# Feed forward in steps of four blocks with half-contraction weight loads, and late attention outputs made transposed

## The reference

```
for layer in range(2):
    x = x + mixer(rms_norm(x))                    # layer 0: sliding window + latent (MLA); layer 1: dilated
    x = x + memory_cross_attention(rms_norm(x), rms_norm(mem))
    x = x + (silu(h @ w_gate) * (h @ w_up)) @ w_down     # h = rms_norm(x); hidden width 2816
return rms_norm(x)
```

## Time and profile before

| | us |
|---|---|
| Median of 3 runs | 3666.4 (3652.03 to 3669.24) |
| The profiled execution | 3675.72 |
| Its span, first to last instruction | 3673.9 |

### The profile page before, as it was taken

How to read it: one execution, slowest core, us unless ns; L and a number is a source line. 1 busy time by engine, 2 the same in 40 slices (tenths; PEclk the granted TensorE clock), 3 DMA queues, 4 the chain that set the end, 5 groups by cost and what they waited for, 6 DMA issues and landing times. The chain is left out here.

```text
span 3673.9 us, 45086 instructions
## 1 busy us (share of the span) xinstructions
PE 3154.4 (86%) x17286; PEld 2315.8 (63%) x17286; DVE 2008.6 (55%) x4183; ACT 708.2 (19%) x1736; POOL 1343.8 (37%) x1166
## 2 busy tenths in 40 slices
PE   8889988977778787577888887889998999999999
PEld 3566478843334343254667776677875788877887
DVE  2341355489898888777776688776544210133201
ACT  2231221222121111113220013210023210122100
POOL 0840032156776777653455555455300000000000
PEclk9998999988889889877899999899999999999999
DMA  6422100289999999976899999899831244422343
GB/s 216 129 75 72 46 3 5 66 295 357 367 370 358 385 371 393 357 275 232 285 344 390 393 386 347 298 349 390 330 95 35 69 143 155 139 91 81 115 149 103
DMA packets 420396, 832.17 MB, mean 227 GB/s; under 512 B 40467, under 2 KB 258510, under 8 KB 420174
## 3 DMA queue, kind: packets, MB, share of 16 engines
q0 software_dynamic: 147456, 536.94, 39.1%
q1 hardware_dynamic: 272726, 292.35, 24.3%
HBM read 827.02 MB, written 2.17 MB: 226 GB/s over the span
## 5 line engine op out<-in xcount | busy, mean ns | idle before, releaser
L2822 PE MATMUL banks<-arena 128*128 128x256 f32 (+1 forms) x4736 | 1078.7, 387 | 63.6 <-DMA arena<-in_l_w_up 32.7
L2822 PEld LDWEIGHTS banks<-arena 128*128 128x128 f32 (+1 forms) x4736 | 909.6, 194 | 218.3 <-DMA arena<-in_l_w_up 36.3
L2369 POOL DMA_INDIRECT arena<-in_peer_v,arena x512 | 583.9, 1140 | 399.9 <-DVE arena L2485 233.8
L2369 POOL DMA_INDIRECT arena<-in_peer_u,arena x512 | 571.8, 1117 | 425.6 <-DVE arena L2499 147.4
L2499 DVE CUSTOM_DVE_ANT_0 arena<-arena 128x1024 f32<-128x1024 f32 x512 | 628.2, 1227 | 114.0 <-DMA arena<-in_peer_u,arena 72.1
L2441 PE MATMUL banks<-arena 128*128 128x512 f32 x768 | 419.3, 689 | 189.0 <-DMA arena<-in_peer_v,arena 67.9
L2485 DVE SCALAR_TENSOR_TENSOR arena<-arena 128x1024 f32<-128x1024 f32 x316 | 406.2, 1286 | 31.6 <-DMA arena<-in_peer_v,arena 13.1
L2441 PEld LDWEIGHTS banks<-arena 128*128 128x128 f32 x768 | 159.9, 219 | 405.2 <-issue 314.2
L3787 PE MATMUL banks<-arena 128*128 128x256 f32 x1408 | 310.5, 378 | 0.0
L3836 DVE TENSOR_TENSOR arena<-banks,arena 128x512 f32<-128x512 f32 x44 | 30.5, 693 | 498.3 <-PE banks L2822 495.6
L3787 PEld LDWEIGHTS banks<-arena 128*128 128x128 f32 x1408 | 265.7, 189 | 38.3
(11 more groups left out here) (313 smaller groups left out, 3416.6 us busy)
## 6 DMA issues: line engine op xcount, KB each, us to landing
arena<-in_l_w_gate SPq DMA_DIRECT2D x44, 1024.0 KB
arena<-in_l_w_up SPq DMA_DIRECT2D x44, 1024.0 KB
arena<-in_l_w_down SPq DMA_DIRECT2D x44, 1024.0 KB
arena<-in_ada_w SPq DMA_DIRECT2D x24, 1024.0 KB, 7.6
arena<-in_l_w_qkv SPq DMA_DIRECT2D x24, 1024.0 KB
arena<-in_w_in SPq DMA_DIRECT2D x33, 512.0 KB, 4.0
arena<-in_l_w_out SPq DMA_DIRECT2D x16, 1024.0 KB
arena<-in_peer_q_w SPq DMA_DIRECT2D x10, 1024.0 KB
```

The lines of the kernel that those rows point to most:

```text
L2369: p.e.indirect_dma_start(e.ring[slot], None, tables[table], bass.IndirectOffsetOnAxis(ap=e.IDX[h][:, t, j:j + 1], axis=0)).then_inc(*p.up( ...
L2822: ins = p.e.matmul(out, left(c), right(c), start=c == 0, stop=c == c_n - 1, skip_group_check=True)
```

## The change

The feed forward goes in steps of blocks: (0), (1,2), (3,4), ... (9,10). For a step of two blocks, gate and up weights come as two loads each: rows 0 to 511 and rows 512 to 1023 of 512 columns (runs of 2 KB). Gate uses banks 0 and 1, up banks 2 and 3. The order is g0 u0 | g12 u12 d0 | g34 u34 d1 d2 | ... | d9 d10. Silu is written to `a.hid[i % 4]` and multiplied in place; `a.sg` goes.

In half 1 the units have an order of their own (`late_order`). The outputs of both heads of a pair are made together after the weights of the next pair's first unit, with the values stationary (64 columns, or 128 for the cross attention) and the transposed weights moving, into partitions 0 to 63 and 64 to 127 of bank 5: the result is already transposed. The reciprocal of the sum is spread over partitions by a matmul of the broadcast column with the identity into bank 4, ACT copies it to `a.O`, DVE multiplies bank 5 with it straight into `a.o`. The transposing store, DVE's scaling per unit and its copy go.

```
-        a.hid, a.sg = F.take(2, T), F.take(T)
+        a.hid = F.take(4, T)
...
+def late_order(units):
+    n, former = len(units), None
+    yield "scores", 0
+    for u in range(n):
+        paired = both_halves(units, u + 1)
+        if u + 1 < n and not paired:
+            yield "scores", u + 1
+        yield "fill", u
+        if paired:
+            yield "scores", u + 1
+        yield "weights", u
+        if units[u].c0 == 0 and former is not None:
+            yield "outputs", former
+        if units[u].ends:
+            former = u
+        yield "pause", u
+    yield "rest", 0
+    yield "outputs", former
...  (units_pe)
+        elif step == "outputs":
+            if filled < 4 * MM:
+                occupied(k, p, a, 1, 5)
+            p.wait_ge(*x.values_at)
+            p.claim(("bank", 5), S.dve_stored, key)
+            group = group_of(units, u)
+            for v in group:
+                p.wait_ge(weights_by(k, a, v), (name, v))
+            for j in range(len(x.values)):
+                for v in group:
+                    y = units[v]
+                    ins = p.e.matmul(k.bank[5][y.c0:y.c0 + y.w, 0:P], y.values[j], a.PT[v % 2][:, j * P:j * P + P], start=j == 0,
+                                     stop=j == len(x.values) - 1, skip_group_check=True)
+                    if j == len(x.values) - 1:
+                        ins.then_inc(*p.up(S.output_filled, (name, v)))
+            p.wait_ge(S.vector_step, ("inverted", *key))
+            p.claim(("bank", 4), S.act_scaled, key)
+            for v in group:
+                y = units[v]
+                ins = p.e.matmul(k.bank[4][y.c0:y.c0 + y.w, 0:P], a.small[:, v % 4, 4:5].to_broadcast([P, y.w]), k.ident,
+                                 start=True, stop=True, skip_group_check=True)
+            ins.then_inc(*p.up(S.store_filled, key))
...  (units_act)
+        elif step == "outputs":
+            if x.tile in stored:
+                p.wait_ge(S.dve_stored, stored[x.tile])
+            p.wait_ge(S.store_filled, key)
+            p.e.activation(a.O[x.tile], k.bank[4][:, 0:P], ACT.Copy).then_inc(*p.up(S.act_scaled, key))
+            stored[x.tile] = key
...  (units_dve)
+        elif step == "weights" and a.late:
+            if weights_by(k, a, u) is S.dve_weights:
+                if u >= 2:
+                    p.wait_ge(S.output_filled, (name, u - 2))
+                p.wait_ge(S.weights_filled, key)
+                p.e.tensor_copy(a.PT[1][:, 0:x.m], k.bank[4][:, 0:x.m]).then_inc(*p.up(S.dve_weights, key))
+            p.wait_ge(S.weights_exp, key)
+            if x.sink is not None or 0 < x.nb < x.m:
+                p.e.tensor_tensor(cols[:, 2:3], cols[:, 2:3], cols[:, 3:4], ALU.add).then_inc(*p.up(S.vector_step))
+                p.in_order()
+            p.e.reciprocal(cols[:, 4:5], cols[:, 2:3]).then_inc(*p.up(S.vector_step, ("inverted", *key)))
+        elif step == "outputs":
+            p.wait_ge(S.output_filled, key)
+            p.wait_ge(S.act_scaled, key)
+            p.e.tensor_tensor(x.dst, k.bank[5][:, 0:P], a.O[x.tile], ALU.mult).then_inc(*p.up(S.dve_stored, key))
...
+FFN_STEPS = [(0,)] + [(2 * q + 1, 2 * q + 2) for q in range((NH // 2 - 1) // 2)]
+GATE, UP = (0, 1), (2, 3)
+def rows_half(w, c0, r):
+    return lambda slot: [(slot.rearrange("p (c n) -> p c n", n=T), columns(w, c0, T)[:, 4 * r:4 * r + 4, :])]
...  (ffn_sp)
+            for r in range(2):
+                load_wide(k, p, (name, l, h, step[0], r), rows_half(w, 256 * step[0], r), over=(name, l, h, step[-1], r))
...
+def quad_pe(k, p, a, l, name, step, banks, emptied, norm):
+    for r in range(2):
+        w = landed_wide(k, p, (name, l, h, step[0], r)).rearrange("p (c n) -> p c n", n=T)
+        for x in range(4):
+            i, b = step[x // 2], banks[x // 2]
+            if r == 0 and x % 2 == 0:
+                p.claim(("bank", b), emptied, (l, h, i))
+            for c in range(4):
+                p.wait_ge(S.normed, (norm, 4 * r + c))
+                ins = p.e.matmul(k.bank[b][:, x % 2 * TH:x % 2 * TH + TH], w[:, c, P * x:P * x + P], a.h[:, 4 * r + c, :],
+                                 start=r == 0 and c == 0 and x % 2 == 0, stop=r == 1 and c == 3, skip_group_check=True)
...
+            yield 4 * MM
...  (ffn_act, ffn_dve, for i in step)
+            if i >= 4:
+                p.wait_ge(S.proj_filled, ("down", l, h, i - 4))
+            p.e.activation(a.hid[:, i % 4, :], k.bank[GATE[bank_of(step, i)]], ACT.Silu).then_inc(*p.up(S.gate_silu, (l, h, i)))
...
+            p.e.tensor_tensor(a.hid[:, i % 4, :], k.bank[UP[bank_of(step, i)]], a.hid[:, i % 4, :], ALU.mult).then_inc(
+                *p.up(S.hidden_ready, (l, h, i)))
```

More of the change, by code:

```diff
@@ L3074, in rest, with group_of, unit_order @@
         yield from self.take(10**6, 10**6)
-def unit_order(units):
+def late_order(units):
[16 more added lines that the diff above has]
+    yield "outputs", former
+def group_of(units, u):
+    return (u,) if units[u].w == P else (u - 1, u)
+def unit_order(units, late):
+    if late:
+        yield from late_order(units)
+        return
     n = len(units)
@@ L3156, in units_pe @@
     S, filled, made = k.S, 0, set()
-    for step, u in unit_order(units):
+    for step, u in unit_order(units, a.late):
         x, key = units[u], (name, u)
@@ L3231, in units_act @@
             p.e.activation(a.PT[u % 2][:, 0:x.m], k.bank[4][:, 0:x.m], ACT.Copy).then_inc(*p.up(S.act_weights, key))
-        elif step == "output" and a.h_id == 0:
+        elif step == "output":
             if x.c0 == 0 and x.tile in stored:
@@ L3240, in units_act @@
                 stored[x.tile] = key
-        elif step == "store" and stored_by(k, a, x.tile) is S.act_stored:
+        elif step == "outputs":
[4 more added lines that the diff above has]
+            stored[x.tile] = key
+        elif step == "store":
             p.wait_ge(S.store_filled, key)
@@ L3246, in units_dve @@
 def units_dve(k, p, a, name, units, fill, rate):
-    S, stored = k.S, {}
-    for step, u in unit_order(units):
+    S = k.S
+    for step, u in unit_order(units, a.late):
         x, key = units[u], (name, u)
@@ L3288, in units_dve @@
             p.in_order()
[L3289 to L3299, removed]
-                stored[x.tile] = key
-        elif step == "store" and stored_by(k, a, x.tile) is S.dve_stored:
-            p.wait_ge(S.store_filled, key)
-            p.e.tensor_copy(x.dst, k.bank[4][:, 0:P]).then_inc(*p.up(S.dve_stored, key))
+            p.e.reciprocal(cols[:, 4:5], cols[:, 2:3]).then_inc(*p.up(S.vector_step, ("inverted", *key)))
 def rotate_act(k, p, a, j, src, scale, key, rows=P, made=None):
```

165 lines of the change are left out of this document (89 added, 76 removed).

## The result

| | before | after |
|---|---|---|
| median of runs | 3666.4 us (11 runs) | 3641.3 us (11 runs) |
| profiled execution, its span | 3675.7, 3673.9 us | 3644.5, 3642.6 us |
| ratio after / before | | 0.993, 95% interval 0.9911 to 0.995 |

What follows compares the result with a forecast made beforehand. It took TensorE (86% busy) as the main bound, with saturated DMA engines in half 0's feed forwards. Packets -8, DMA sharing -9 and attention 0 sum to -17, for a median of 3649 us, range 3618 to 3690.

Steps and rivals of the forecast that it cites:

- Feed forward, half 0: packets of 2 KB: Half 0's feed forwards: larger weight packets save 4 us each, so -8, bounds 0 and -12.
- Rival C: Half 0's feed forwards don't move, being bound by bytes and DVE's order: 3666 us, chance 0.11.
- Feed forward, half 0: who gets the DMA engines: Half 0: first feed forward 0 beyond packets; second pulls work into its late gap, -9, bounds 0 and -12.
- Rival D: Half 0: weights' larger DMA share lets TensorE run through both feed forwards, -46 in all: 3620 us, chance 0.12.
- Attention, half 1: Half 1's attention: savings and new costs sum to 0, bounds -20 and +35.
- Output products, -17: Half 1's attention: outputs in two column halves overlap, as the scores' row halves do, saving 17 us; if not, 0.
- Rival A: Half 1's attention: column halves run one after the other, so the -17 goes: 3666 us, chance 0.13.
- Store transposes, -33: Half 1's attention: 48 store transposes, the waits ahead of them and 8 us of waits ahead of dummies go.
- New wait for bank 4: Half 1's attention: the broadcast waits until ACT has copied the next unit's transposed weights out of bank 4, +25 us.
- Array modes, +6: Half 1's attention: changes between full and half columns cost 0.1 us each way, +6, bounds 0 and +19.
- The terms +14, +8 and -3: Half 1's attention: spread reciprocals +14 us, pairs without fill +8, fewer dummies -3.
- Rival B: Half 1's attention: the outputs step blocks TensorE, without overlap and with a lower clock: 3688 us, chance 0.20.

Runs made afterwards that it cites:

- att_only: The kernel before with only the attention part of the change: 3657.9 us, ratio 0.9981.
- more_dummies: The kernel before with three dummy matmuls instead of one where the fill has run out in half 1's attention: 3692.2 us, ratio 1.009.
- half_down: The changed kernel with half of the bytes of half 0's down weights (blocks 0 to 9) not loaded: 3620.6 us, ratio 0.9888.
- packets_1k: The changed kernel with each 1 MB gate and up load as two of 512 KB, in runs of 1 KB: 3662.2 us, ratio 0.9992.
- bank5: The changed kernel with the broadcast of the reciprocals in free columns of bank 5 instead of bank 4: 3598.8 us, ratio 0.9817.
- heads_serial: The changed kernel with a pair's output products made head by head instead of alternating column halves: 3640.7 us, ratio 0.9919.
- bank5_serial: bank5 with a pair's output products made head by head: 3614.9 us, ratio 0.987.

## Why the prediction was right or wrong

**Total.** Forecast -17, measured -25. The sign and the place were right: the gain is in the second feed forward of half 0, and its cause is the larger runs of the weights. The size came out near because the errors of two terms went against each other: the first feed forward gave about 2 us or none where -4 stood, and the second gave -21 where -13 stood, beyond the bounds of its term. How near it came is in part luck.

**Feed forward, half 1: nothing.** Right. A step of two blocks, 128 products of gate and up and 64 of down, takes 41.5 us against 2 x 20.77.

**Feed forward, half 0: packets of 2 KB.** Packet count as predicted. The saving of -4 per feed forward was worked out as less time on the engines. The rate did rise as that says, from 393 to 402 GB/s in both saturated stretches. But in the first feed forward the two profiles show nothing of it: over the stage the rate went from 385 to 393 GB/s while its length stayed, 270.1 and 270.2. By queue, the gathers brought 69.8 MB in both, the weights' queue 34.2 MB before and 36.2 after: the gain went into 2 MB of weights that came earlier than they were needed. Over all profiles the stage is 270.1, 273.2 and 272.8 us with the old feed forward (before, *att_only*, *more_dummies*) and 269.5 to 270.6 with the new one and whole loads (six kernels), so about -2 instead of -4. Rival C holds for this feed forward, and only for it.

**Feed forward, half 0: who gets the DMA engines.** For the first, "a faster TensorE only waits for DVE at the end: 0" was the right mechanism, with 17.8 + 14.5 us of new waits in place of 26.3 old ones and the clock at 0.93 instead of 0.98; *half_down* shows that bytes set its length. That the two profiles agree to 0.1 us is chance. For the second the mechanism was right (weights early, gathers pulled into the gap behind 2620 us) and the size wrong: -9, with the -4 for packets -13, against -21. The missing 8 us are mostly the clock. The whole stage, before:

```profile
2406.00:2669.00 263.00, 242.88 (x1063) 207.89 (x1064) 164.54 (x197) 22.70 (x30) 128.20 (x111) 0.95 0.97 358
```

and after:

```profile
2404.00:2646.00 242.00, 234.54 (x1067) 203.59 (x1066) 164.11 (x197) 21.64 (x29) 127.84 (x111) 0.98 1.01 388
```

TensorE's busy time fell from 242.9 to 234.5 us for the same products, with the granted clock at 0.95 and 0.98, and its idle time from 20.1 to 7.5. I had read this cost in the earlier trace rows, 10.2 us for 32 instructions behind a wait instead of 7.1, and then priced the removed waits by their length alone. A removed wait also gives back the slow products behind it. Here this belongs to the change and not to chance: the sum of 10 us x (1 - clock) over this stage is 8.5 to 13.7 us in the four kernels with runs of 1 KB and 3.4 to 5.1 in the six with runs of 2 KB and whole loads. Of Rival D, the part for the second feed forward came true and more; the first couldn't follow, since it is bound by bytes.

The steps of four blocks, to which I gave a share of the gain ("meets TensorE in six places instead of eleven"), have none that shows by themselves: *packets_1k* keeps them and is at 3662.

**Attention, half 1.** Its sum of 0 was nearly right; at full clock, about -2 in layer 0's attention and -0.4 in the dilated one, whose clock is 1.00 in both kernels. How near to 0 it came is in part luck, since the terms that the traces can check are off in both directions:

- Output products, -17: the overlap is real, but its price isn't a term of a sum. Outputs are busy 29.7 us against 54.9, and from the first of 16 to the broadcast it is 0.93 us in *bank5*, where I expected nine slots, 0.96. *heads_serial* shows that with the wait in place the overlap gave nothing, because the copy was released by the first head alone. So Rival A's price of +17 was wrong too: without the overlap the time would have been the same.
- Store transposes, -33: they and their waits are gone, but 8 us of this were waits ahead of dummies, of which TensorE still has 8.1 us (before: 10.2), now mostly for DVE's copy of the odd units' weights.
- New wait for bank 4, +25: 22.3 us listed. That is a right number for what the waits list, but the price was 33 us in the stages: the lost pipelining at each group's end comes on top. The saving of the overlap (9 us, *bank5_serial*) was inside the 22.3.
- The wait for L3297 is gone, as predicted. Array modes, +6: right. Each change between full and half columns costs 0.09 us in *bank5*, where I took 0.1, twice for each of 32 pairs: 6 us. The Trainium skill ("TensorEngine Tiling (Array Packing)", "Tiling Modes") says that TensorE drains when the tiling mode changes; the traces agree that a change costs something, these 0.09 us.
- The terms +14, +8 and -3 were not measured one by one; the dummies went from 176 instructions to 146, as -3 says.
- Clock, taken as 0: it was 5 us in the profiled executions, of a quantity that varies by 7 between kernels with the same attention. The rows before had no way to size it, so it belonged in the range.
- Rival B didn't come: an outputs step of 16 with its broadcast takes 2.1 us, far from the 3 that it needed.
- Half 1's attention stretches are given as 356 us together; the two of the table of stages are 166 and 146, 312.

What I missed is that a gain larger than all that the change gave lay beside it: free columns of bank 5 for the broadcast. The prediction named the wait, priced it at 25 us, and accepted it.

## What to carry to other kernels

Where two queues keep the DMA engines full, look at the size of the packets in each: here larger runs for the weights gave their queue more of the engines, TensorE's waits vanished and came back on DVE, and the time fell only in the stage that wasn't bound by bytes. Price a wait on TensorE with the slower clock behind it. A shorter group of products is worth something only if what comes next waits for its end: find the one instruction that releases the next step before you count a saving. And when a new wait is in the price of a change, look first for another bank or free columns.

## What the runs showed that was not expected

- Packets of 2 KB instead of 1 KB in the weights' queue, beside gathers of rows in packets of 3.6 KB on average, moved TensorE's waits for weights from 44 us to 0 over the two feed forwards and DVE's for rows to 147 us, while the total rate rose by 2% only (393 to 402 GB/s).
- fp32 products in alternating column halves: 16 in 1.10 us, head by head 1.59 us.
- A change between full and half columns of the array: 0.20 us from start to start where the same products without a change have 0.11.
- A listed wait of 0.67 us on TensorE between two groups of small products costs 0.84 us from start to start.
- The clock's sum in the same stage of kernels with the same attention ranges from 1.7 to 8.5 us. Kernels with the same feed forward have medians within 5 us of one another (3637.2, 3640.7, 3641.3) with runs spread over 16 to 23 us. Differences in one stage of one profile below some 7 us need the clock taken out first.
